# Four pairs' tokens gathered at once in a two-layer mixture-of-experts trunk, two weight homes given back in quarters, part of one last weight loaded ahead

## The reference

```python
# 512 tokens, D_MODEL 1024, D_EXPERT 512, N_EXPERTS 32, TOP_K 2, all float32
x = x + hierarchical_moe(rms_norm(x, ln_ffn[layer]), ...)   # once in each layer
...
def expert_block(args):            # xb: the rows of the tokens routed to expert e
    xb, e = args
    hid = jax.nn.silu(xb @ w_gate[e]) * (xb @ w_up[e])
    return hid @ w_down[e]
...
y = jnp.zeros((n_tok, d), x.dtype).at[tok_sorted].add(y_rows[dest] * gate_sorted[:, None])
```

## Time and profile before

| | |
|---|---|
| median of 3 runs | 1673.77 us (1672.04 to 1674.14) |
| profiled execution: its time, its span | 1674.34 us, 1672.4 us |
| TensorE busy | 1641.0 us (98%) |
| VectorE, ScalarE, GpSimd busy | 679.7, 410.8, 225.9 us |
| moved by DMA | 460.85 MB |
| experts of layer 0, of layer 1 | about 313 to 776 us, about 1204 to 1665 us |

### The profile page before, as it was taken

The page is one execution under the profiler, slowest core; times in us unless marked ns, Lnnn a source line. Parts: engine busy times, 40 slices in busy tenths (PEclk is TensorE's granted clock), DMA queues, the critical chain, the costliest instruction groups (busy, mean ns, idle before and its releaser), DMA issues.

```text
span 1672.4 us, 22380 instructions
## 1 busy us (share of the span) xinstructions
PE 1641.0 (98%) x9377; PEld 1054.2 (63%) x9377; DVE 679.7 (41%) x1238; ACT 410.8 (25%) x766; POOL 225.9 (14%) x162
## 2 busy tenths in 40 slices
PE   7999899999999999999999999999999999999997
PEld 7878788645445454536888888888754544545443
DVE  4887864533433243334413223242623342324333
ACT  4576663300000000004332414223500000000000
POOL 1600101000000000003444344432100000000000
PEclk9999999999999999999999999999999999999999
DMA  9420222799999999997313122223499999999996
GB/s 207 106 51 1 66 90 101 329 421 425 423 428 426 425 426 423 427 423 286 105 51 101 65 87 101 91 84 140 194 421 427 426 423 427 426 426 425 425 426 268
DMA packets 77655, 460.85 MB, mean 276 GB/s; under 512 B 6768, under 2 KB 32592, under 8 KB 51312
## 3 DMA queue, kind: packets, MB, share of 16 engines
q1 hardware_dynamic: 76816, 457.03, 67.3%
q0 software_dynamic: 736, 2.34, 1.2%
HBM read 457.25 MB, written 2.10 MB: 275 GB/s over the span
## 4 chain that ended last, share of the span: by engine, by line
PE 93%; DVE 2%; DMA 2%; ACT 2%; issue 1%; SPq 0%; DVEq 0%; ACTq 0%
PE bank L161 31%; PE bank L1953 26%; PE bank L1971 13%; PE bank L1911 7%; PE bank L1978 7%; DMA ring<-in_w_down_dram 1%; PE bank L1962 1%; PE bank L1617 1%; DMA ring<-in_w_in_even_dram 1%; PE bank L1904 0%; PE bank L2515 0%; PE bank L2628 0%; PE bank L1936 0%; PE bank L1605 0%; PE bank L1030 0%
## 5 line engine op out<-in xcount | busy, mean ns | idle before, releaser
L1953 PE MATMUL bank<-ring,SCR 128*64 128x512 f32 x1776 | 445.5, 592 | 0.8 <-issue 0.8
L161 PE MATMUL bank<-ring_r 128*128 128x512 f32 (+2 forms) x1120 | 337.5, 380 | 1.7 <-DVE ring_r L443 1.7
L1953 PEld LDWEIGHTS bank<-ring,SCR 128*64 128x64 f32 x1776 | 146.1, 137 | 249.2 <-issue 248.7
L161 PEld LDWEIGHTS bank<-ring_r 128*128 128x128 f32 x1120 | 206.1, 188 | 41.4 <-issue 3.1
L1971 PE MATMUL bank<-ring,SCR 128*64 128x512 f32 x880 | 226.9, 595 | 0.1
L1945 DVE SCALAR_TENSOR_TENSOR X<-bank,AU,X 128x512 f32<-128x512 f32 x256 | 173.8, 744 | 88.9 <-PE bank L1978 88.9
L1990 DVE TENSOR_TENSOR SCR<-SCR,bank 128x512 f32<-128x512 f32 x32 | 22.0, 688 | 361.0 <-PE bank L1953 361.0
L1971 PEld LDWEIGHTS bank<-ring,SCR 128*64 128x64 f32 x880 | 70.1, 137 | 121.6 <-issue 121.6
L161 PE MATMUL bank<-ring_r,SCR_r 128*128 128x512 f32 x576 | 138.5, 395 | 0.0
L2484 POOL TENSOR_TENSOR ring_r<-ring,ring_r 128x1024 fp32r<-128x1024 f32 x48 | 116.9, 2470 | 143.6 <-ACT ring_r L2470 143.6
L1978 PE MATMUL bank<-SCR_r 128*128 128x512 f32 x512 | 131.9, 400 | 0.3 <-DVE SCR_r L1987 0.3
(11 more groups left out here) (463 smaller groups left out, 1870.7 us busy)
## 6 DMA issues: line engine op xcount, KB each, us to landing
ring<-in_w_gate_dram SPq DMA_DIRECT2D x55, 2048.0 KB, 15.4
ring<-in_w_up_dram SPq DMA_DIRECT2D x52, 2048.0 KB, 18.3
ring<-in_w_down_dram SPq DMA_DIRECT2D x51, 2048.0 KB, 15.7
ring<-in_w_in_odd_dram SPq DMA_DIRECT2D x8, 2048.0 KB, 9.3
SCR<-in_w_gate_dram SPq DMA_DIRECT2D x9, 1024.0 KB, 12.0
SCR<-in_w_down_dram SPq DMA_DIRECT2D x9, 1024.0 KB, 18.2
ring<-in_w_in_even_dram SPq DMA_DIRECT2D x16, 512.0 KB, 6.5
SCR<-in_w_up_dram SPq DMA_DIRECT2D x8, 1024.0 KB, 15.4
```

The costliest lines, as they stand in the source:

```text
L161: mm = pe.matmul(out, lhs[a], rhs[b], start=(first and i == 0), stop=(last and i == 2))
L1953: mm = pe.matmul(bank[SLOTS * u:SLOTS * u + SLOTS, :], xt[:, k, SLOTS * u:SLOTS * u + SLOTS], w[u](k), start=(k == 0), stop=(k == KT - 1))
```

## The change

It has three parts.

1. `OH` becomes 512 columns wide and `XT` a single buffer for a quad, four pairs. Pairs 0 and 1 still gather 256 columns each (pairs 2 and 3's tokens, into the right half of the first quad). From then on a gather is 512 columns wide, one k-tile to a bank: pairs 2 and 3 gather four k-tiles of the next quad each, in two turns, the second of them between the combine and `down`, and pairs 4 to 11 two k-tiles each. Pairs 12 to 15 gather nothing. The copies of a quad are written where the pair just read had its tokens, so the layout of `XT` alternates from quad to quad (`xt_quad`).
2. The weights n = 7 and 8 are loaded in quarters (512 KB). Their old homes are given back after every second k-tile of the gate of pair 0 (`first_gate`).
3. The first 1,536 columns (768 KB) of n = 92, the last pair's first up matrix, are loaded before them, into free scratch (`AHEAD`), and that weight's later load is shorter by as much.

```diff
+        IN_QUARTERS = (E_SLOTS, E_SLOTS + 1)
+        AHEAD_ROWS = 3
...
-        OH = tg(r32(s_(NT * DUO)))
+        QUAD = 4 * P
+        OH = tg(r32(s_(NT * QUAD)))
...
-        XT = [s_(KT * DUO).rearrange("p (k n) -> p k n", k=KT) for _ in range(2)]
+        XT = s_(KT * QUAD)
+        XT_k = XT.rearrange("p (k n) -> p k n", k=KT)
...
+        def xt_quad(k, quad):
+
+            if quad % 2 == 0:
+                return XT_k[:, k, :].rearrange("p (j s) -> p j s", j=4)
+            return XT.rearrange("p (j b c s) -> p j b c s", j=4, b=2, c=4)[:, :, k % 2, k // 2, :]
+
+        def xt_quad_copy(dve, l, bank, k, quad):
+            return dve.tensor_scalar(xt_quad(k, quad), bank[:, :].rearrange("p (j s) -> p j s", j=4), gcol[:, l, k:k + 1], None, ALU.mult)
...
+        def gathers(i):
+
+            if i < 2:
+                return [(2 * i,), (2 * i + 1,)]
+            if i < 4:
+                k = 4 * (i - 2)
+                return [(k, k + 2), (k + 1, k + 3)]
+            return [(2 * (i % 4),), (2 * (i % 4) + 1,)] if i < PAIRS - 4 else [(), ()]
...
-                    ready = [(0, mw("xt_out", 2 * i + 4 if duo_after(i) else NE))]
-                hidden_mm(pe, BG, range(2), w_two(l, 0, i, KT), x_of(n), ready).then_inc(ms("gate"), 1)
+                    ready = [(0, mw("xt_out", gathered(i) - 1)), (KT - 2 if i == 2 else KT - 1, mw("xt_out", gathered(i)))]
+                quarters = {k: sg("first_gate") for k in (1, 3, 5)} if is_at(i, 0) else {}
+                hidden_mm(pe, BG, range(2), w_two(l, 0, i, KT), x_of(i), ready, quarters).then_inc(ms("gate"), 1)
...
                 if before:
                     combine(i - 1, 1 - b, range(4, 8))
+                if i in (2, 3):
+                    for half in range(2):
+                        gather(i, n, half, 1)
...
-                if b == 0 and duo_after(i):
-                    dve.wait_ge(*mw("gat", 2 * i + 4))
-                    one_hots(4 * (d + 1), 4).then_inc(ms("oh"), 1)
+                if is_at(i, 0):
+                    one_hots(4, 4, DUO).then_inc(ms("oh"), 1)
+                elif is_at(i, 2) or n == 0 and gathers(i)[0]:
+                    dve.wait_ge(*mw("gat", gathered(i)))
+                    one_hots(8 * (i // 4 + 1), 8).then_inc(ms("oh"), 1)
...
+                if i in (2, 3):
+                    adds(i - 1, range(4))
                     for half in range(2):
-                        x_out(2 * i + 4 + half, BX[half], 1 - n // 2, 2 * b + half)
+                        x_out(i, half)
+                    adds(i - 1, range(4, 8))
+                    for half in range(2):
+                        x_out(i, half, 1)
...
+            def load_quarter(n, a):
+                quarter = slice(a * SLOT // 4, (a + 1) * SLOT // 4)
+                sp.dma_start(ring[:, home(l, n), quarter], source(n)[:, quarter]).then_inc(w_landed[home(l, n)], 16)
+
             for n in FIRST_LOADS[l]:
                 load(n)
-            for n in range(E_SLOTS, tail):
+            for at in ahead_release(l):
+                sp.wait_ge(*at)
+            sp.dma_start(AHEAD, source(tail)[:, 0:AHEAD_ROWS * 512]).then_inc(first_half(tail % 6), 16)
+            for a in range(4):
+                sp.wait_ge(*((sg("first_gate"), 3 * l + a + 1) if a < 3 else mw("gate", 1)))
+                for n in IN_QUARTERS:
+                    load_quarter(n, a)
+            for n in range(E_SLOTS + 2, tail):
                 load(n)
```

More of the change, by code:

```diff
@@ L253, in expert_landings @@
         def expert_landings(l, s, n):
-            return len(weight_pieces(s)) * sum(home(l, m) == s for m in range(n))
+            return sum(4 if m in IN_QUARTERS else len(weight_pieces(s)) for m in range(n) if home(l, m) == s)
         def landed(c):
@@ L1952, in hidden_mm, with x_of @@
                 for u in us:
-                    mm = pe.matmul(bank[SLOTS * u:SLOTS * u + SLOTS, :], xt[:, k, SLOTS * u:SLOTS * u + SLOTS], w[u](k), start=(k == 0), stop=(k == KT - 1))
-            return mm
-        def x_of(n):
-            return XT[n // 2][:, :, n % 2 * P:n % 2 * P + P]
+                    mm = pe.matmul(bank[SLOTS * u:SLOTS * u + SLOTS, :], xt(k)[:, SLOTS * u:SLOTS * u + SLOTS], w[u](k), start=(k == 0), stop=(k == KT - 1))
+                if k in read:
+                    mm.then_inc(read[k], 1)
+            return mm
+        def x_of(i):
+            return lambda k: xt_quad(k, i // 4)[:, i % 4, :]
         def ht_mm(pe):
@@ L2016, in all_pairs, with gathered @@
                 pair(i, i % 4, i // 2)
-        def duo_after(i):
-            return not isinstance(i, int) or i < PAIRS - 2
+        def gathers(i):
[5 more added lines that the diff above has]
+            return [(2 * (i % 4),), (2 * (i % 4) + 1,)] if i < PAIRS - 4 else [(), ()]
+        def gathered(i):
+            return 4 + sum(len(a) for j in range(i) for a in gathers(j))
         def is_at(i, n):
@@ L2072, in combine, with gather @@
                     comb_mm(pe, comb_bank(m), m, b).then_inc(ms("comb"), 1)
[L2074 to L2079, removed]
+            def gather(i, n, half, turn=0):
+                at = gathered(i) + 2 * turn + half
+                if half + turn == 0 and (i in (0, 2) or i >= 4 and n == 0):
+                    pe.wait_ge(*mw("oh", {0: 2, 2: 3}.get(i, 3 + i // 4)))
+                pe.wait_ge(*(mw("xt_out", at - 1) if turn else mw(("sil", "hh")[half], i + 1)))
+                k = gathers(i)[half][turn]
+                if i < 2:
+                    gather_mm(pe, BX[half], (2 * k, 2 * k + 1), DUO, first=DUO).then_inc(ms("gat"), 1)
+                else:
+                    gather_mm(pe, BX[half], (k,), QUAD).then_inc(ms("gat"), 1)
             def slots_placed(i, b):
@@ L2231, in of_experts, with one_hots, x_out @@
                 return cols[:, :, :, None].to_broadcast([P, NT, e, SLOTS])
-            def one_hots(first, e):
-                return dve.tensor_tensor(by_expert(OH[:, :, 0:e * SLOTS]), slots(e), of_experts(POSM, first, e), ALU.is_equal)
-            def x_out(n, bank, buf, q):
-                dve.wait_ge(*mw("gat", n + 1))
-                xt_copy(dve, l, bank, buf, (2 * q, 2 * q + 1), DUO).then_inc(ms("xt_out"), 1)
+            def one_hots(first, e, at=0):
+                return dve.tensor_tensor(by_expert(OH[:, :, at:at + e * SLOTS]), slots(e), of_experts(POSM, first, e), ALU.is_equal)
+            def x_out(i, half, turn=0):
+                if gathers(i)[half]:
+                    k = gathers(i)[half][turn]
+                    dve.wait_ge(*mw("gat", gathered(i) + 2 * turn + half + 1))
+                    if i < 2:
+                        out = xt_copy(dve, l, BX[half], (2 * k, 2 * k + 1), DUO, DUO)
+                    else:
+                        out = xt_quad_copy(dve, l, BX[half], k, i // 4 + 1)
+                    out.then_inc(ms("xt_out"), 1)
             def placed(i, b):
@@ L2303, in pair @@
                     placed(i, b)
-                adds(i - 1, range(8))
-                if duo_after(i):
+                if i in (2, 3):
+                    adds(i - 1, range(4))
                     for half in range(2):
-                        x_out(2 * i + 4 + half, BX[half], 1 - n // 2, 2 * b + half)
+                        x_out(i, half)
+                    adds(i - 1, range(4, 8))
+                    for half in range(2):
+                        x_out(i, half, 1)
+                else:
+                    adds(i - 1, range(8))
+                    for half in range(2):
+                        x_out(i, half)
                 y_out(i)
@@ L2332, in experts_dve @@
                         for half in range(2):
-                            xt_copy(dve, l, BX[half], 0, range(4 * half, 4 * half + 4), P)
+                            xt_copy(dve, l, BX[half], range(4 * half, 4 * half + 4), 0, P)
                         ot_ones(dve, 0, place_over).then_inc(over_done(l, "v_xt_out"), 1)
```

39 lines of the change are left out of this document (24 added, 15 removed).

## The result

| | before | after |
|---|---|---|
| median (lowest to highest) of 5 runs | 1673.77 us (1672.04 to 1674.45) | 1683.09 us (1680.73 to 1684.03) |
| ratio, 95% interval | | 1.0060 (1.0048 to 1.0071) |
| profiled execution: its time, its span | 1674.34, 1672.4 us | 1683.09, 1681.1 us |
| gate of pair 0 to gate of pair 15, layer 0 and layer 1 | 431.9 and 431.7 us | 436.8 and 436.8 us |

The change costs 9.3 us, 0.6%; 1682.2 had been forecast. The last line of the table, from the starts of the gates in TensorE's timeline, is the yardstick of this study: it grew by 4.9 + 5.1 us, where the span grew by 8.7 (between the layers 1.0 is won, and 0.3 outside the two stretches at the start and the end).

The account below looks back on a forecast made before the run. The load stream was taken to bound the kernel, weight 91's landing starting pair 15. Layer shifts of 4.2 and 4.4 us, less 0.2 for the part loaded ahead, made 8.4 us: 1682.2 us forecast, range 1674 to 1687 (8 in 10).

Parts of the forecast that it names:

- What bounds the kernel: Expert stages: the DMA, slower by 0.58 us a pair, decides; pair 15 starts when weight 91 lands, in both layers.
- The wide gathers: TensorE: 1.9 us less work a layer, but pairs 2 and 3 grow by 3.52 us each, 7.04 together.
- The rival by which wide matmuls cost like narrow ones: Gather matmuls of 512 columns take about 0.12 us, so no change: 1671.2 us; chance 0.12, together with cases of half the delay.
- Where the delay meets the stream: n = 29, behind `down` of pair 3: issued 7.04 us later, landing 4.2 us later in layer 0, 4.4 in layer 1.
- the two places named: Layer 0, near 401 and 434 us, as `down` of pairs 2 and 3 ends: DMA share falls below 0.7.
- Nothing later can catch up: Load stream from n = 29 to n = 91: full at 4.958 us a weight, so the shift at n = 29 stays.
- Quarters: Opening, first gate: quarters of homes come back from about 315.3 us, every 1.7 us; value at the end nothing.
- The opening gain: n = 8 ends about 1 us earlier in layer 0, about 5 in layer 1.
- the part ahead: 768 KB, 1.9 us of the stream, loaded in layer 0's opening where the queue would be dry; saves some 0.2 us.
- VectorE: Pairs 2 and 3: copies ready before TensorE's second turn, hidden by 1 us; if not, 1.4 us in each pair.
- TensorE's busy time: New profile of layer 0: TensorE's busy time is 3.8 us less.
- The sum: Whole kernel: 4.2 + 4.4 - 0.2 = 8.4 us slower.

Follow-up runs that it names:

- e5_drop23: e2_wide with 14 of the 16 matmuls of the gather's second turn left out in pairs 2 and 3; 1672.01 us, ratio 0.9997 to the kernel before.
- e12_delay: The kernel before with 15 idle matmuls of 512 columns ahead of `down` of pairs 2 and 3; 1682.76 us, ratio 1.0061.
- e4_drop3: e2_wide with 14 of the 16 matmuls of the gather's second turn left out in pair 3 alone; 1677.65 us, ratio 1.0027 to the kernel before.
- e3_behind: The changed kernel with the gather's second turn of pairs 2 and 3 moved behind `down`; 1682.62 us, ratio 1.0052 to the kernel before.
- e9_all_halves: e8_halves with halves in the opening too and nothing loaded ahead; 1681.81 us, ratio 1.0060 to the kernel before.
- e8_halves: The changed kernel with `down` of pairs 0 to 13 by rows, homes given back in halves (1,024 KB loads); 1680.20 us, ratio 1.0046 to the kernel before.
- e2_wide: The changed kernel with only part 1, the wide gathers; 1682.51 us, ratio 1.0055 to the kernel before.
- e11_small_loads: The kernel before with every full load into the ring issued as four of 512 KB together; 1705.21 us, ratio 1.0195.

## Why the prediction was right

**What bounds the kernel.** Right. n = 91 decides when pair 15 starts, before and after, and e5_drop23 shows that TensorE's time saved ahead of it is worth nothing. Time added is another matter: TensorE is only 1.0 and 0.8 us from being the bound in the kernel before, and in e12_delay it is.

**The wide gathers.** Right. Eight of 512 columns take 1.82 to 1.85 us (1.84 had been taken from the combine). The second turn is 3.63 us, pairs 2 and 3 take 32.60 us (32.7), pair 12 takes 25.4 (25.3). The rival by which wide matmuls cost like narrow ones falls: 0.23 us each. The 131 ns of the Trainium skill (TensorE: Matmul & The Clock Gate, Back-to-back issue gap) are not met in this stream.

**Where the delay meets the stream.** Right at n = 29: 6.9 us late in its issue (7.0 forecast), 4.1 and 4.7 in its landing in the two layers (4.2 and 4.4 forecast), dips to 0.69 and 0.50 of the DMA share at the two places named. Three things were missed. First, pair 2 alone puts n = 28 2.5 and 2.6 us late where 1 us was forecast: a weight close behind the restart lands late by itself, in layer 0 n = 24 (6.3 us after n = 23), in layer 1 n = 27 (6.1 after n = 26). That is hidden at n = 29, which waits for its home anyway, and shows in e4_drop3. Second, the lateness doesn't stay as it is at n = 29. "Nothing later can catch up, since the stream is full at 4.958 us a weight" takes an average for a pace. In the full stream a weight lands 4.9 us after the one before it, and in each layer of these traces some land 0.3 to 1.6 us late: n = 43, 49 and 88 in layer 0 of the kernel before (5.3, 5.6 and 6.2 us), n = 57, 74 and 79 in the changed one (5.3, 5.3 and 5.6). So 4.1 and 4.7 us at n = 29 become 6.0 and 5.0 at n = 36 and 4.9 and 5.1 at pair 15. Third, the delay was said to act because it stands ahead of `down`. That is one of its ways only: e3_behind and e9_all_halves, and e8_halves in layer 0, show that the gate of pair 4 can charge the same lateness again.

**Quarters.** The end value, nothing, was right. The opening gain was mis-sized: in layer 0 n = 8 lands at 333.2 against 333.1, not 1 us earlier, and in layer 1 2.9 us earlier, not 5, of which 0.4 is left at n = 11. The first and the last of the eight issues, 315.37 (of n = 7) and 320.89 (of n = 8), us to landing:

```profile
ring<-in_w_gate_dram SPq DMA_DIRECT2D x1, 512.0 KB, 8.6
...
ring<-in_w_up_dram SPq DMA_DIRECT2D x1, 512.0 KB, 12.3
```

They land at 324.0 and 333.2, seven gaps of 1.31 us in the mean. The queue is full from 318 to 324 us now (DMA share 1.00, where it was 0.55), but the part ahead, which had been taken to fall into free time, has its 1.9 us in the same queue, and 512 KB loads are slow ones. In layer 0 n = 9 to 12 land 0.6 to 0.7 us earlier than before, which n = 29 can't pass on.

**VectorE.** Right: the second turn follows the combine without a gap (388.85 + 1.81 = 390.66), and its two halves follow each other without one (16 matmuls in 3.63 us).

**TensorE's busy time.** Off: 3.8 us less were forecast and 2.1 came. The 32 matmuls of the up of pair 14 in layer 1 are drawn out to 8.78 us from 7.09: some standing still is counted as busy there, and 1.7 us is the size of the miss. The waits that the timeline shows add up to 7.5 us in layer 0 (7 forecast) and 5.9 in layer 1.

**The sum.** 4.9 + 5.1 - 1.0 - 0.3 = 8.7 us of span, 8.4 forecast. The two errors, the shift 1.4 us too small and a microsecond won between the layers that had not been forecast, nearly cancel, and that is luck: the second may be no more than the spread of single executions, since the kernels here have 456.0 to 458.4 us between the gate of pair 15 and the next layer's first gate, with no pattern. The kernel before has the longest of them.

**Open.** Why single weights land late in a full stream, and why it is n = 24 in layer 0 (6.3 to 6.4 us after n = 23) and n = 27 in layer 1 (5.6 to 6.1 us after n = 26) in all four kernels whose `down` of pair 2 is late for the gather or the idle matmuls alone (after, e2_wide, e12_delay, e4_drop3). What idle matmuls in a late pair would cost in the changed kernel, where TensorE waits 7.5 and 5.9 us ahead of pair 15: nothing up to about that much by the argument here, but no run has them.

## What to carry to other kernels

Where a full load stream and a full engine run side by side, find the weight whose landing starts the last stage, and follow it back to the place where the stream is thinnest; extra work there is paid for less what the queue still holds (6.9 us cost 4.9 and 5.1 here), and savings behind it bring nothing. Look too at how far the other resource is from being the bound, here 1.0 and 0.8 us of TensorE. Count the homes before giving them back in smaller pieces: with seven homes for six weights a pair, the homes of the next pair repeat the lateness. And gather work forward into the early pairs at most by as much as the issue-to-landing time there stands above that of a dry queue, read at each pair that grows (10.1 against 7.7 us at n = 23, 10.5 at n = 29); e4_drop3, 3.5 us over in pair 2 alone, still lost 2.6 us of the stream.

## What the runs showed of the hardware

A queue of 512 KB loads moves 410 GB/s where 2,048 KB loads move 425 and 426, at the same full share, also with four issued back to back (e11_small_loads). In a full stream of 2,048 KB loads one lands 4.9 us after the other, but some in each layer take 5.2 to 6.5 us (n = 88 of the kernel before 6.2 and 6.1 us, n = 50 in layer 1 of e5_drop23 6.4). A load of 2,048 KB issued with at most 2.1 us of older work in the queue takes 7.3 to 8.6 us (n = 23 and 29 in the changed kernel, e2_wide and e12_delay, both layers). The first load of an expert stage, into an empty queue, mostly takes 7.6 to 8.0 us, but 8.6 in layer 0 of e12_delay and 9.7 in layer 1 of e5_drop23. That 2.7 us of older work hide a start doesn't hold throughout: with 2.9 us n = 23 in layer 0 of the changed kernel lands 4.9 us after the weight before it, but n = 24 then 6.3 us later; with 2.4 us n = 31 of e3_behind takes 7.2 (with 3.1 us in layer 1, 6.8); with 3.2 us n = 31 takes 6.4 in e8_halves and 5.6 in e9_all_halves, layer 0. With 4.1 and 4.2 us n = 11 of the kernel before lands 4.9 us after n = 10.
